# The first recurrent tile's gate products move into the four quarters of the array

## The chip, the core and the metric

The kernel runs on one NeuronCore of one Trainium2 chip. The metric is device time in microseconds (us) of one launch. A core has a matrix engine (TensorE, PE in the rows, with its weight loads as PEld), a vector engine (VectorE, DVE), a scalar engine (ScalarE, ACT), GpSimd (POOL), and a queue engine (SyncE, SP) that here only waits on semaphores and issues transfers. The five work through their own instruction lists in order and meet at semaphores.

## The reference

One layer of a hybrid decoder is computed for a prompt of 512 + 16 tokens and 8 sample streams of 8 tokens (592 token columns in all). What bears on this change is the recurrent branch:

```python
z = xn @ w_in + b_in                  # u = first 1024 columns of z
uc, _ = causal_dwconv(u, ...)         # width-4 depthwise convolution
xb = uc.reshape(B, L, 16, 64)         # 16 blocks of 64 channels
r = sigmoid(einsum('blnc,ncd->blnd', xb, w_r) + b_r)
i = sigmoid(einsum('blnc,ncd->blnd', xb, w_i) + b_i)
a = exp(-8 * r * softplus(-lam))
inp = sqrt(1 - a*a) * (i * uc)
h[t] = a[t] * h[t-1] + inp[t]         # a scan over the tokens
```

Everything else (an mLSTM branch, the merge, a ConvFFN of 2 x 2816 columns, norms) follows, and most of the time lies in its dense products.

## The kernel before

**Layout.** Features lie on the 128 partitions, tokens along the free dimension. The 1024 recurrent channels are 8 tiles u(0) to u(7) of 128 channels, each tile two of the 16 blocks. A dense product of one tile of 128 output columns (`gemm`, `split_product`) is 48 matmuls: 8 slices of the contraction, three terms each (weight high x input high, high x low, low x high), two halves of the tokens.

**Weights.** Each tile's 512 KB of weights goes through three steps. SP loads it into one of two slots of `stage` (`load`, line 569); ACT writes its rounded high part to `whi` (line 985); POOL subtracts to get the low part in `wlo` (line 927) and raises `w_lo`. Weight tile b = g + 1 belongs to the dense tile g. SP loads weight tile b only when `w_lo` says that b - 2 is split (the slot is then free). ACT takes its work in a fixed order: high part of the weight tile for g + 2, then the eviction of tile g into `u` (lines 1174 and 1176), then its share of the recurrent branch. PE starts tile g when `w_lo` counts its weights and the tile before last is evicted.

**The gates.** When u(p) is evicted, DVE convolves it into `uc[:, p]` (lines 1555 to 1560, raising `conv_done`). PE then computes the two gate products of the tile in `lru_gates(p)`, put in just ahead of dense tile `LRU_TURN[p]` (3 for p = 0, 6 for p = 1). The weights are block-diagonal, two 64 x 64 blocks per tile, in the tiles `bd[0]` (r) and `bd[1]` (i). For p = 0 the whole 128 x 128 array is used, with zeros off the diagonal: four matmuls in the code (two gates, two halves of 308 columns), which appear as eight in the trace. For p >= 1 four 64 x 64 products run side by side: the two blocks of r on the diagonal quarters, from `uc`, and the two blocks of i on the off-diagonal quarters, which take their input from a copy of `uc[:, p]` with its two halves of 64 partitions exchanged (`us[p % 2]`). The i weights of tiles 1 to 7 are therefore stored off the diagonal in `bd[1]`, those of tile 0 on it.

**The copies.** `swap_halves(p)` on SP waits until `uc[:, p]` is there, and issues two transfers (lines 660 and 661). SP's loop over g issues the weight load `main_load(g)` first (for g > 2), and then the copy whose `LRU_SWAP[p]` is g. `LRU_SWAP` is (0, 6, 7, 9, 12, 14, 16, 18), and the inner loop begins at p = 1. `main_load(3)` brings the weights (b = 4) of dense tile 3, `main_load(4)` those of tile 4, and so on. Ahead of this loop SP has stored `x_raw` to DRAM (line 636).

**PE's order in the stretch in question:** dense tiles u(1), u(2), then `lru_gates(0)`, then u(3), u(4), u(5), `lru_gates(1)`, u(6).

Of the kernel before, what the change touches and what calls it, by code (L numbers as in the profile page):

```python
# [118 lines left out]
LRU_EXP = (4, 7, 10, 12, 14, 16, 18, 20)  # L119
LRU_ROOT = (5, 8, 12, 14, 16, 18, 21, 21)  # L120
LRU_SPLIT = (6, 9, 13, 15, 17, 19, 22, 23)
LRU_SWAP = (0, 6, 7, 9, 12, 14, 16, 18)
U0 = LW - 1
US = U0 + TP
UGR = LW - 1 + LS
# [2 lines left out]
UH = UN // 2  # L128
# [124 lines left out]
def hybrid_layer(nc, a, o):  # L253
    w_in, b_in = a["w_in"][0], a["b_in"][0]
    ctx = ExitStack()
    with ctx:
        base = 16512

        def sb(name, shape, off, dt=F32):
            return nc.alloc_sbuf_tensor_at(name, shape, dt, offset=base + off)  # L260

        def sem(name):
            return ctx.enter_context(nc.semaphore(name))
# [53 lines left out]
        bd = [sb("lru_w_r", [P, 8, P], o_h + SB + 32 * UW), sb("lru_w_i", [P, 8, P], o_p + 512 * NROW + 1024)]  # L317
        uc = sb("uc", [P, 8, UN], r)
# [124 lines left out]
        bank = ctx.enter_context(nc.psum_tensor("bank", [P, 4, 512], F32))  # L443
# [18 lines left out]
        def bank2(s):  # L462

            return bank[:, 2 * s:2 * s + 2].rearrange("p h t -> p (h t)")
# [21 lines left out]
        def ffn_out(n):  # L486
# [23 lines left out]
        us_in = [sem("us_in0"), sem("us_in1")]  # L510
        bd_in, negc_ready = sem("bd_in"), sem("negc_ready")
        bd_zero, conv_done, lru_ps, lru_sig, lru_exp, lru_q, lru_sq, lru_h, lru_hi, lru_lo_ = (
            sem("bd_zero"), sem("conv_done"), sem("lru_ps"), sem("lru_sig"), sem("lru_exp"), sem("lru_q"),
            sem("lru_sq"), sem("lru_h"), sem("lru_hi"), sem("lru_lo"))
# [37 lines left out]
        def aview(ap):  # L552
            return ap.rearrange("(r c) -> r c", c=P)
# [9 lines left out]
        def _(sp):  # L563
# [39 lines left out]
            def params(arrived, group):  # L603

                for rtile, r0, src in group:
                    sp.dma_start(rows[r0:r0 + src.shape[0], rtile], src).then_inc(arrived, 16)
# [3 lines left out]
            for hf in range(2):  # L610
                lo_, hi_ = slice(BW * hf, BW * hf + BW), slice(BW - BW * hf, 2 * BW - BW * hf)
                wr, wi = (a[n][0].rearrange("(p two) c d -> two c p d", two=2)[hf] for n in ("lru_w_r", "lru_w_i"))
                sp.dma_start(bd[0][lo_, :, lo_], wr).then_inc(bd_in, 16)
                sp.dma_start(bd[1][lo_, 0:1, lo_], wi[:, 0:1]).then_inc(bd_in, 16)
                sp.dma_start(bd[1][hi_, 1:8, lo_], wi[:, 1:8]).then_inc(bd_in, 16)
            params(rows_in[1], ((1, 0, aview(a["lru_lambda"][0])), (1, 8, aview(a["mlstm_head_g"][0])),
                    (1, 16, a["state_lru_h"][0].rearrange("b (f c) -> (b f) c", c=P)),
                    (2, 0, a["state_mlstm_n"][0].rearrange("b h (i c) -> (b h i) c", c=P)),
# [24 lines left out]
            def main_load(g):  # L643

                b = B_U + g
                sp.wait_ge(w_lo, b - 1)
                if g < 16:
                    c0 = P * g if g < 8 else COL_GA + P * (g - 8)
                    load(b, b % 2, w_in, slice(c0, c0 + P))
                elif g < 24:  # L650
                    c0 = head_col(g - 16)
                    load(b, b % 2, w_in, slice(c0, c0 + P))
                else:
                    load(b, b % 2, a["w_branch_a"][0], slice(P * (g - 24), P * (g - 24) + P))
            def swap_halves(p):

                sp.wait_ge(conv_done, p + 1)
                if p >= 3:
                    sp.wait_ge(lru_ps, p - 1)
                sp.dma_start(us[p % 2][0:BW, :], uc[BW:P, p]).then_inc(us_in[p % 2], 16)  # L660
                sp.dma_start(us[p % 2][BW:P, :], uc[0:BW, p]).then_inc(us_in[p % 2], 16)

            for g in range(1, 28):
                if g > 2:
                    main_load(g)
                for p in range(1, 8):
                    if LRU_SWAP[p] == g:
                        swap_halves(p)

# [1406 lines left out]
        def _(pe):  # L2076
# [149 lines left out]
            def lru_gates(p):  # L2226

                pe.wait_ge(conv_done, p + 1)
                if p:
                    pe.wait_ge(lru_sig, p)  # L2230
                else:
                    pe.wait_ge(bd_in, 96)
                    pe.wait_ge(tile_evicted, T_U + 1)
                if p == 0:
                    for g in range(2):
                        for hf in range(2):
                            last = pe.matmul(bank[:, 2 * g + hf, 0:UH], bd[g][:, p, :], uc[:, p, UH * hf:UH * hf + UH],
                                             start=True, stop=True)
                    last.then_inc(lru_ps, 1)
                    return  # L2240

                pe.wait_ge(us_in[p % 2], 32 * ((p + 1) // 2))
                A, B = slice(0, BW), slice(BW, P)
                for hf in range(2):
                    c_ = slice(UH * hf, UH * hf + UH)
                    for g, k_, m_ in ((0, A, A), (0, B, B), (1, A, B), (1, B, A)):
                        x_ = us[p % 2][k_, c_] if g else uc[k_, p, c_]
                        last = pe.matmul(bank[m_, 2 * g + hf, 0:UH], bd[g][k_, p, m_], x_, start=True, stop=True,  # L2248
                                         tile_position=(k_.start, m_.start), skip_group_check=True)
                last.then_inc(lru_ps, 1)  # L2250

            for g in range(1, 16):
                if g in LRU_TURN:
                    lru_gates(LRU_TURN.index(g))
                gemm(B_U + g, T_U + g, (B_U + g) % 2, (T_U + g) % 2, KT, xh, xl, m0=0 if g < 8 else M0,
                     free=T_COLS2 + 1 if g == 1 else None)
# [20 lines left out]
            for n in range(8):  # L2277
                if 16 + n in LRU_TURN:
                    lru_gates(LRU_TURN.index(16 + n))
                fill(0, n)  # L2280
            for f in range(8):
# [8 lines left out]
                elif f == 6:  # L2290
                    pe.wait_ge(gates_ready, 1)
                    pe.wait_ge(lc_ready, 1)
                    for b_, r0 in ((2, 32), (3, 96)):
                        for c in range(TT):
                            last = pe.transpose(bank[:, b_, 4 * c:4 * c + HEADS], gq[r0:r0 + HEADS, P * c:P * c + P],
                                                ident[r0:r0 + HEADS, r0:r0 + HEADS])
# [187 lines left out]
            for h in range(2):  # L2484
# [17 lines left out]
                for m in range(2, 8):  # L2502
                    ffn_begin(d0 + m)
                    down_steps(m, range(HK)).then_inc(tile_done, 1)
                    if h and m == 2:

                        pe.wait_ge(tile_evicted, T_FFN + d0 + 1)
                        for n in range(FC):
                            ft, w_ = FC_SET * n, 18 * min(FC_SET, UPT - FC_SET * n)
                            last = pe.transpose(bank2(0)[0:w_, P * n:P * n + P],  # L2510
                                                flast[:, ft:ft + w_ // 18].rearrange("p f r -> p (f r)"), ident[:, :])
# [67 lines left out]
```

## Time and profile before

| | us |
|---|---|
| median of 3 runs (1062.61 to 1063.84) | 1062.91 |
| the profiled execution's own time | 1062.86 |
| its span, first to last instruction | 1061.0 |
| PE busy in the span | 1049.6 |
| DVE busy | 638.0 |
| ACT busy | 386.0 |
| POOL busy | 371.1 |

The execution whose trace is read took 1062.86 us, 1.86 us more than its span. All times in rows are counted from the start of the span. In a timeline a line gives the start, the time from there to the end of the last of the merged instructions, the engine, the line of the kernel, what is written and read, and how many instructions were merged; in brackets stands idle time before it and what ended that. SPq lines are issues of transfers: their duration is that of the issue, not of the transfer, which lands later.

### The profile page before, as it was taken

To read this page: it belongs to the slowest core of one execution; us is meant where nothing else is said; L and a number is where in the kernel's file an instruction comes from. 1 tells how busy PE (TensorE), PEld (TensorE's weight loads), DVE (VectorE), ACT (ScalarE), POOL (GpSimd) and SP (SyncE) were. 2 spreads that over 40 slices of the span, in tenths; PEclk is the share of its full clock that TensorE was granted. 3 is DMA by queue.
4 is the path that set the end of the run, shared out by engine and by line. 5 is a ranking of instruction groups with operands and counts; after the bars stand their busy time and mean duration, and the time that the engine had idled before them with its cause. 6 is when DMAs were issued, how large, how long until landed. Compare 5 with 4: busy or idle time off the path is not lost.

```text
span 1061.0 us, 19369 instructions
## 1 busy us (share of the span) xinstructions
PE 1049.6 (99%) x7924; PEld 1024.7 (97%) x7924; DVE 638.0 (60%) x975; ACT 386.0 (36%) x558; POOL 371.1 (35%) x180
## 2 busy tenths in 40 slices
PE   7999999999999999999999999999999999999997
PEld 6999999999999999999999999999999999999997
DVE  6777457964544463363643339999940189999313
ACT  6566787313333334222422343222211122222332
POOL 4333343333222222232133334444433333334430
PEclk9999999999999999999999999999999999999999
DMA  8443332376487595783452233222323222333312
GB/s 198 156 112 92 96 80 80 99 191 163 86 231 202 136 261 128 190 231 90 149 172 82 80 100 100 80 80 80 103 82 95 60 81 80 85 94 97 96 44 90
DMA packets 246465, 126.08 MB, mean 119 GB/s; under 512 B 67916, under 2 KB 242236, under 8 KB 246127
## 3 DMA queue, kind: packets, MB, share of 16 engines
q1 hardware_dynamic: 246172, 124.82, 42.8%
q8 instruction: 63, 1.03, 0.4%
q14 instruction: 20, 0.16, 0.1%
q10 hardware_dynamic: 210, 0.07, 0.0%
HBM read 100.62 MB, written 22.04 MB: 116 GB/s over the span
## 4 chain that ended last, share of the span: by engine, by line
PE 98%; ACT 1%; POOL 1%; issue 0%; DVE 0%; POOLq 0%; DVEq 0%
PE ring L2091 48%; PE ring L2480 23%; PE bank L2480 17%; PE bank L2351 2%; PE bank L2338 1%; PE bank L2138 1%; PE bank L2319 1%; PE bank L2331 1%; PE bank L2392 1%; PE bank L2248 1%; PE bank L2380 1%; POOL x_split L939 0%; PE bank L2112 0%; PE bank L2526 0%; ACT x_raw L1037 0%; ACT sq_tok L1022 0%
## 5 line engine op out<-in xcount | busy, mean ns | idle before, releaser
L2091 PE MATMUL ring<-x_split,whi 128*128 128x256 f32 (+1 forms) x2016 | 358.6, 299 | 0.0
L927 POOL TENSOR_TENSOR wlo<-stage,whi 128x1024 fp32r<-128x1024 f32 x78 | 194.8, 2497 | 405.6 <-ACT whi L985 405.6
L2091 PEld LDWEIGHTS ring<-x_split,whi 128*128 128x128 f32 x2016 | 304.3, 189 | 8.1 <-issue 7.6
L2091 PE MATMUL ring<-x_split,wlo 128*128 128x256 f32 (+1 forms) x1008 | 217.5, 297 | 0.0
L2091 PEld LDWEIGHTS ring<-x_split,wlo 128*128 128x128 f32 x1008 | 169.9, 189 | 0.0
L985 ACT ACTIVATE whi<-stage 128x1024 fp32r<-128x1024 f32 x80 | 84.3, 1053 | 97.0 <-PE ring L2091 81.0
L970 POOL TENSOR_TENSOR wlo<-stage,whi 128x1024 fp32r<-128x1024 f32 x28 | 71.1, 2539 | 108.6 <-ACT whi L1321 108.6
L2480 PE MATMUL ring<-x_split,whi 128*128 128x256 f32 (+1 forms) x512 | 88.7, 295 | 0.0
L1437 DVE SCALAR_TENSOR_TENSOR conv<-up,cols,conv 128x592 f32<-128x592 f32 x88 | 75.5, 858 | 3.1
L2480 PEld LDWEIGHTS ring<-x_split,whi 128*128 128x128 f32 x512 | 77.0, 189 | 0.0
L1997 DVE TENSOR_SCALAR conv<-up,cols 128x592 f32<-128x592 f32 x44 | 68.4, 1554 | 3.1
L2480 PE MATMUL bank<-x_split,whi 128*128 128x256 f32 (+1 forms) x384 | 66.5, 295 | 0.0
L970 POOL TENSOR_TENSOR wlo_third<-stage,whi_third 128x1024 fp32r<-128x1024 f32 x16 | 40.8, 2550 | 58.7 <-ACT whi_third L1321 58.7
L2480 PEld LDWEIGHTS bank<-x_split,whi 128*128 128x128 f32 x384 | 57.7, 189 | 0.0
L1357 ACT ACTIVATE conv<-conv 128x592 f32<-128x592 f32 x22 | 15.4, 700 | 116.3 <-DVE conv L1437 116.3
L973 POOL TENSOR_TENSOR wlo<-stage,whi 128x1408 fp32r<-128x1408 f32 x12 | 38.7, 3228 | 52.6 <-ACT whi L1323 52.6
L2480 PE MATMUL ring<-x_split,wlo 128*128 128x256 f32 (+1 forms) x256 | 54.7, 296 | 0.0
L1321 ACT ACTIVATE whi<-stage 128x1024 fp32r<-128x1024 f32 x28 | 29.5, 1054 | 61.2 <-PE ring L2480 40.4
L1838 DVE COPY num_tok<-bank 128x257 f32<-128x257 f32 x20 | 8.5, 426 | 68.7 <-PE bank L2338 60.6
L2041 DVE TENSOR_TENSOR resid<-ring,resid 128x576 f32<-128x576 f32 x9 | 6.8, 758 | 68.9 <-PE ring L2480 68.9
L2480 PE MATMUL ring<-x_split,whi_third 128*128 128x256 f32 (+1 forms) x256 | 44.6, 296 | 0.0
L2480 PE MATMUL bank<-x_split,whi_third 128*128 128x256 f32 (+1 forms) x256 | 44.4, 295 | 0.0
(364 smaller groups left out, 2063.2 us busy)
## 6 DMA issues: line engine op xcount, KB each, us to landing
stage<-in_w_in SPq DMA_DIRECT2D x56, 512.0 KB, 4.3
stage<-in_w_up SPq DMA_DIRECT2D x44, 512.0 KB, 3.8
stage<-in_w_down SPq DMA_DIRECT2D x16, 704.0 KB, 4.4
stage<-in_w_branch_a SPq DMA_DIRECT2D x8, 512.0 KB, 3.8
c_sample<-in_state_mlstm_C SPq DMA_DIRECT2D x16, 256.0 KB, 6.8
out_s_mlstm_C<-c_sample SPq DMA_DIRECT2D x16, 256.0 KB, 2.4
stage<-in_w_branch_b SPq DMA_DIRECT2D x8, 512.0 KB, 4.0
stage<-in_w_out SPq DMA_DIRECT2D x8, 512.0 KB, 3.7
```

Of the source, the lines that this page charges most:

```text
L927: pool.tensor_tensor(spaced(wlo[:, slot]), packed(stage[:, slot, 0:n]), spaced(whi[:, slot]).bitcast(F32), ALU.subtract).then_inc(w_lo, 1)
L970: pool.tensor_tensor(spaced(l_), packed(stage[:, b % 2, 0:D]), spaced(w_).bitcast(F32), ALU.subtract).then_inc(w_lo, 1)
L973: pool.tensor_tensor(l_, stage[:, b % 2, :], w_.bitcast(F32), ALU.subtract).then_inc(w_lo, 1)
L985: act.activation(spaced(whi[:, slot]), packed(stage[:, slot, 0:n]), ACT.Copy).then_inc(w_hi, 1)
L1321: act.activation(spaced(ffn_weight(i)[0]), packed(stage[:, b % 2, 0:D]), ACT.Copy).then_inc(w_hi, 1)
L1357: act.activation(cv[:, 1, 0:CV_N], cv[:, 1, 0:CV_N], ACT.Gelu_apprx_tanh).then_inc(gelu_done, 1)
L1437: return stt(out=out, in0=in0, scalar=scalar, in1=in1, op0=op0, op1=op1)
L1997: st.link(ts(c_, U[:, 0:CV_N], w[0], bias, ALU.mult, ALU.add))
L2091: last = pe.matmul(of(z, t0 or -2, t1), w[:, kk * WS:kk * WS + P], x_, start=kk == 0 and m == 0, stop=kk == kn - 1 and m == 2)
L2138: last = pe.matmul(of_first(z, t0, t1)[0:M], w[:, step * kk:step * kk + M], x[:, f, t0:t1], start=kk == 0 and m == 0, stop=kk == KT - 1 an ...
L2351: lz = pe.matmul(ZP[:, ii], kw[kappa % 3][:, P * ii:P * ii + P], vt[s][:, c, :], start=True, stop=True, skip_group_check=True)
L2480: last = pe.matmul(out(z, t0, t1), w_[:, kk * step:kk * step + P], x_[:, kk, t0 - at:t1 - at], start=kk == 0 and m == 0, stop=kk == kn - 1 ...
```

## The change

`lru_gates(0)` takes the form of the others: for each of the two halves of the tokens four quarter products, from `uc` and from a copy with exchanged halves in `us[0]`. So the copy of tile 0 is now made, at `LRU_SWAP[0] = 2`. Since `main_load` begins at g = 3, these two transfers, and the wait for `uc[:, 0]` ahead of them, stand in SP's list before `main_load(3)`. The i weights of tile 0 move off the diagonal, so that each half of `bd[1]` is loaded by one transfer instead of two (`bd_in` counts to 64, not 96). The copy of tile 2, which uses the same `us[0]` as tile 0, now waits until the gates of tile 0 are done, and the counts on `us_in` follow.

```diff
-LRU_SWAP = (0, 6, 7, 9, 12, 14, 16, 18)
+LRU_SWAP = (2, 6, 7, 9, 12, 14, 16, 18)
...
                 sp.dma_start(bd[0][lo_, :, lo_], wr).then_inc(bd_in, 16)
-                sp.dma_start(bd[1][lo_, 0:1, lo_], wi[:, 0:1]).then_inc(bd_in, 16)
-                sp.dma_start(bd[1][hi_, 1:8, lo_], wi[:, 1:8]).then_inc(bd_in, 16)
+                sp.dma_start(bd[1][hi_, :, lo_], wi).then_inc(bd_in, 16)
...
                 sp.wait_ge(conv_done, p + 1)
-                if p >= 3:
+                if p >= 2:
                     sp.wait_ge(lru_ps, p - 1)
...
             for g in range(1, 28):
                 if g > 2:
                     main_load(g)
-                for p in range(1, 8):
+                for p in range(8):
                     if LRU_SWAP[p] == g:
                         swap_halves(p)
...
-                    pe.wait_ge(bd_in, 96)
+                    pe.wait_ge(bd_in, 64)
                     pe.wait_ge(tile_evicted, T_U + 1)
-                if p == 0:
-                    for g in range(2):
-                        for hf in range(2):
-                            last = pe.matmul(bank[:, 2 * g + hf, 0:UH], bd[g][:, p, :], uc[:, p, UH * hf:UH * hf + UH],
-                                             start=True, stop=True)
-                    last.then_inc(lru_ps, 1)
-                    return
-
-                pe.wait_ge(us_in[p % 2], 32 * ((p + 1) // 2))
+                pe.wait_ge(us_in[p % 2], 32 * (p // 2 + 1))
```

## Rows read from the trace of the kernel before

**Rows 1.** The page, part 4: the chain that ended last, by engine.

```profile
PE 98%; ACT 1%; POOL 1%; issue 0%; DVE 0%; POOLq 0%; DVEq 0%
```

**Rows 2.** Waits of PE, whole span: waiting line, cause, total us, times, longest.

```profile
PE ring L2107 <- POOL misc L906: 2.9, 1, 2.9
PE bank L2138 <- POOL wlo_third L945: 1.0, 1, 1.0
```

**Rows 3.** Timeline of PE, 47 to 49.6 us: gates of tile 0.

```profile
47.18 0.44 PE L2091 MATMUL ring<-x_split,wlo 128*128 128x272 f32 x2
...
49.30 0.52 PE L2091 MATMUL ring<-x_split,whi 128*128 128x272 f32 x1
```

**Rows 4.** Timeline of PE, 68 to 74 us: gates of tile 1.

```profile
69.02 0.44 PE L2091 MATMUL ring<-x_split,wlo 128*128 128x272 f32 x2
69.38 0.48 PE L2248 MATMUL bank<-uc,lru_w_r 64*64 64x308 f32 x2
...
70.58 0.82 PE L2091 MATMUL ring<-x_split,whi 128*128 128x272 f32 x4
```

**Rows 5.** Timeline of SP: issues of an i load, the store of x_raw, a copy.

```profile
13.57 0.62 SPq L615 DMA_DIRECT2D lru_w_i<-in_lru_w_i  x1
...
24.79 0.36 SPq L636 DMA_DIRECT2D x_turned<-x_raw  x1
...
51.69 0.59 SPq L660 DMA_DIRECT2D uc_swapped<-uc  x1
52.32 0.60 SPq L661 DMA_DIRECT2D uc_swapped<-uc  x1
```

**Rows 6.** Timeline of SP, narrow windows: issues of weights of tiles 3 and 4.

```profile
31.05 0.40 SPq L569 DMA_DIRECT2D stage<-in_w_in  x1
...
38.09 0.37 SPq L569 DMA_DIRECT2D stage<-in_w_in  x1
```

**Rows 7.** Waits of SP, 25 to 60 us.

```profile
SPq L569 <- POOL wlo L927: 32.0, 5, 7.1
```

**Rows 8.** Timeline of DVE, 24 to 120 us: convolutions of u(0), u(1); an idle.

```profile
40.24 2.65 DVE L1437 SCALAR_TENSOR_TENSOR uc<-u,cols,uc 128x616 f32<-128x616 f32 x3
43.04 0.18 DVE L1555 COPY stage<-u 128x27 f32<-128x27 f32 x1
...
60.42 0.80 DVE L1580 TENSOR_TENSOR lru_r<-u 128x616 f32<-128x616 f32 x1 [5.44 <-ACT u L1134]
```

**Rows 9.** Timeline of ACT, 24 to 62 us: high part for tile 3, then eviction of u(1).

```profile
41.15 1.07 ACT L985 ACTIVATE whi<-stage 128x1024 fp32r<-128x1024 f32 x1 [4.63 <-PE ring L2091]
42.11 0.69 ACT L1174 ACTIVATE u<-ring,cols 128x528 f32<-128x528 f32 x1
```

**Rows 10.** Timeline of POOL, 24 to 115 us: low parts for tiles 2, 3 and 7.

```profile
35.66 2.41 POOL L927 TENSOR_TENSOR wlo<-stage,whi 128x1024 fp32r<-128x1024 f32 x1 [4.64 <-ACT whi L985]
42.29 2.87 POOL L927 TENSOR_TENSOR wlo<-stage,whi 128x1024 fp32r<-128x1024 f32 x1 [4.23 <-ACT whi L985]
...
70.68 2.95 POOL L927 TENSOR_TENSOR wlo<-stage,whi 128x1024 fp32r<-128x1024 f32 x1 [3.96 <-ACT whi L985]
```

**Rows 11.** Issue to landing (last number), issues at 45.19, 31.05, 51.27, 51.69, 1.67.

```profile
stage<-in_w_in SPq DMA_DIRECT2D x1, 512.0 KB, 3.8
...
stage<-in_w_in SPq DMA_DIRECT2D x1, 512.0 KB, 5.8
...
stage<-in_w_in SPq DMA_DIRECT2D x1, 512.0 KB, 4.9
uc_swapped<-uc SPq DMA_DIRECT2D x1, 154.0 KB, 4.6
...
x_tok<-in_x_prompt SPq DMA_DIRECT2D x1, 512.0 KB, 5.0
```

**Rows 12.** Stretches: us, PE, PEld, DVE, ACT, POOL busy, granted clock, DMA share, GB/s.

```profile
0.00:5.00 5.00, 2.14 (x10) 2.12 (x11) 1.82 (x2) 1.49 (x2) 3.41 (x19) 1.00 0.58 178
...
45.50:46.00 0.50, 0.50 (x6) 0.50 (x5) 0.47 (x2) 0.00 (x0) 0.00 (x0) 1.00 0.00 0
```

## The prediction

> **What bounds the kernel now.** I read the chain of work that ended last first: 98% of it is PE [rows 1]. So the question for every edit is what it does to PE's order of work, and time saved on another engine is worth nothing by itself. Then the waits of PE: nearly all of its idle time lies in the first 15 us, a first wait of 2.9 us and one of 1.0 us being the longest [rows 2]. From there on PE goes from tile to tile without a gap, so any gap that the change opens ahead of a dense tile is added to the end in full, and any matmul time that it saves there is taken off in full. Last I read the timelines of SP, ACT, POOL, DVE and PE between 24 and 75 us side by side, because the change does not only reshape a product: it puts a wait and two transfers into SP's list ahead of the weights of dense tile 3.
>
> **Part 1, the products themselves.** From the start of the last two dense matmuls ahead of the gates of tile 0 to the first dense matmul behind them is 47.18 to 49.30, 2.12 us [rows 3]. The same distance around the gates of tile 1, which already run in quarters and have the same 308 columns, is 69.02 to 70.58, 1.56 us [rows 4]; what the change of form costs on either side is inside it. The new form is thus worth 2.12 - 1.56 = 0.56 us of PE, if nothing else is late.
>
> **Part 2, the weights' loads.** Two issues of 0.62 us [rows 5] fall away and the bytes stay. What follows on SP comes some 1.3 us sooner, until SP next waits: the store of x_raw at 24.79 waits for ACT's copies, and the weight loads from 31.05 on wait for POOL (five waits, 32.0 us together) [rows 5 to 7]. No wait of PE is ended by any of these transfers [rows 2]. I cost this at 0.
>
> **Part 3, the copy of tile 0 ahead of the load for tile 3.** This is the part that decides. SP now has, right behind the store of x_raw, a wait until uc of tile 0 is complete, then two issues, and only then the load of weight tile 4 for dense tile 3. Before, that load was issued at 31.05, when POOL had freed its slot [rows 6, 7]. Now:
>
> - DVE's convolution of u(0) ends at 40.24 + 2.65 = 42.89 [rows 8]. It depends on nothing that moves. SP reacts within about 0.03 us (POOL ends at 35.66 + 2.41 = 38.07 and SP issues at 38.09 [rows 6, 10]): 42.92.
> - First copy to second copy 0.63 us (51.69 to 52.32), then 0.60 us and a gap of 0.05 [rows 5]: the load is issued at 44.20. It is 13.15 us later than before.
> - Landing. A load with nothing beside it took 3.8 us, one with two copies right behind it 4.9, one that met the tail of the x_raw store 5.8 [rows 11]. Ours has 308 KB of copies ahead and the load for tile 4, whose slot has been free since 38.07, 0.4 us behind it. The nearest row is the x_tok load of 512 KB that stood in a queue with transfers on both sides: 5.0 us [rows 11]. I take 5.0 and keep 3.8 and 5.8 as ends: landed at 49.20.
> - ACT's high part to POOL's start is 41.15 to 42.29, 1.14 us [rows 9, 10]; POOL takes 2.41 us, against 2.95 in its slowest row here [rows 10]; the hand-overs at both ends are 0.02 each. PE can start tile 3 at 49.20 + 0.02 + 1.14 + 2.41 + 0.02 = 52.79.
>
> Before, tile 3 started at 49.30 [rows 3]. The cover that the load had was large: ACT could start on these weights only when PE had left their slot at 41.15 [rows 9], and POOL had them split by 42.29 + 2.87 = 45.16 [rows 10], 4.1 us ahead of need. A delay of 13.15 us uses all of this up and leaves 52.79 - 49.30 = 3.49 us of idle PE. With a landing of 3.8 us it is 2.3; with 5.8 and POOL's 2.95 it is 3.49 + 0.8 + 0.54 = 4.8.
>
> The 0.56 us of part 1 is not to be taken off again: the gates are done within the wait. PE has a wait of its own there, for the copy. The second transfer is issued at 43.55 and a copy beside a load landed in 4.6 us [rows 11], so at 48.15 at the latest. Queued behind this wait on PE is everything else; but the products take 69.38 to 70.58, 1.20 us [rows 4], and end by 49.35, over 3 us ahead of the weights. This wait is hidden by the late load. Without that cover it would cost 49.35 - 49.30 = 0.05 us at worst, and at best the full 0.56 us would be gained.
>
> The Trainium skill has a price for a landing: "DMA: Bandwidth & Descriptors", section "Anatomy of one DMA — SWDGE (gpsimd) path", fits 2.0 us plus the bytes over 436 GB/s, by which I estimate 3.2 us for 512 KB. By it tile 3 would start at 50.99 and the loss would be 1.7 us. The trace has 3.8 us for the undisturbed load, and on another queue than that section's, so the row decides.
>
> **What else stands behind the late load.** ACT's list is fixed: the eviction of u(1), right behind the high part for tile 3 and begun at 42.11 [rows 9], with DVE taking it up at 43.04 [rows 8], now runs from some 50.3 to 51.2. PE asks for it before tile 3, but the low part at 52.79 is later. The load for tile 4 is issued at 44.6 instead of 38.09; its high part follows that eviction and is done near 52.3, its low part near 55.2. PE wants it after tile 3, at 52.8 + 6.6 = 59.4 (three dense tiles fill 49.30 to 69.30 [rows 3, 4]): 4 us to spare, so there is no second gap. DVE starts the convolution of u(1) about 8 us later than its 43.04, at 51.3, and what it then did until its idle before 60.42 took at most 60.42 - 5.44 - 43.04 = 11.9 us [rows 8], so it is through by 63.2. The input that ended that idle comes from ACT behind PE's tile 3 and moves to about 63.9. So DVE is back in step. The copy of tile 1 leaves near 57 and lands near 62, with PE wanting it at 69.38 + 3.5 = 72.9. Everything behind tile 3 then runs as before, 3.5 us later.
>
> **The sum.** The profiled execution took 1062.86 us with a span of 1061.0; the median of the runs is 1062.91, so the two can stand for one another. 1062.86 + 3.49 = 1066.4 us. With the ends of the landing and of POOL's step: 1065.2 to 1067.7.
>
> **Rival A, nothing is late (it ends as no change).** If the weights for tile 3 still arrived in time, the new form would give between +0.05 and -0.56 us: 1062.3 to 1062.9, say 1062.6. For this the load would have to be issued by 49.30 - (3.8 + 0.02 + 1.14 + 2.41 + 0.02) = 41.91 even with the fastest landing, so the convolution of u(0) would have to end near 40.6 instead of 42.89. For it speaks the long cover of 10 us between issue and need; against it, that the convolution alone ends later than this point, with 1.3 us of issues still to come. Chance 0.06.
>
> **Rival B, a short landing.** A load that was issued at 45.19 with nothing queued moved no byte until 46.00 [rows 11, 12], 0.8 us. Behind the copies, with the engines already at work, this start could be hidden: a landing of 3.8 - 0.8 = 3.0 us, a loss of 3.49 - 2.0 = 1.5 us, 1064.4 us, which is inside 0.2%. Against it speaks that the copies take engine time themselves, and that no weight load in the rows is under 3.8 us. Chance 0.10.
>
> **Rival C, the clock.** The granted clock is 1.00 in every stretch that I looked at, the 2.4 GHz level, even in the first 5 us where PE was busy for 2.14 us only [rows 12]. The longest idle of PE, 2.9 us, stands ahead of its first matmul [rows 2]. The change leaves PE idle from its gates (48.7 to 49.35) to 52.8, 3.4 to 4.1 us in one piece, behind dense work; the trace has no such place. If the clock falls to 1.2 GHz, dense work takes twice as long until it rises. Between no matmul and the whole of tile 3 at that level the price is 0 to 6.6 us; I take half the tile, 3.3 us: 1066.4 + 3.3 = 1069.7 us. The Trainium skill, "TensorE: Matmul & The Clock Gate", section "HAM oscillation — how this bites in real kernels", describes just that: a wait between bursts of matmuls sends the clock back to the low level. No row here shows it. Chance 0.10.
>
> **How the numbers follow.** The forecast has the remaining 0.74. About 0.2%, 2.1 us, is what a measurement of this kernel can tell from no change; 1065.0 is that point. The forecast's own range, 1065.2 to 1067.7, is above it; rival C too: slower 0.84. Rivals A and B lie within: 0.15, and 0.01 is left for faster. The range that should hold the time 8 times in 10 reaches from rival B's 1064.4 to the forecast's upper end, 1067.8, and leaves out rivals A and C and a rest of the forecast.
>
> **What would show it.** On SP the two copies at 42.9 and 43.5 and the load for tile 3 near 44.2 (instead of 31.05); on ACT an idle until about 49.2 that a transfer ends, then the high part, with the eviction of u(1) behind it; on PE two new idle times, a short one ahead of the gates or none, and one of over 3 us ahead of tile 3 that POOL's low part ends; the gates in 1.2 us. From tile 4 on the distances between tiles should be the old ones. The prediction is wrong if the idle ahead of tile 3 is under 2 us, if a second gap follows at tile 4, 5 or at the gates of tile 1, or if the granted clock is under 1.00 behind the idle.

## The result and the profile after

The changed kernel took 1066.97 us (median of 6 runs, 1065.72 to 1069.14) against 1062.87 us before (6 runs): a ratio of 1.004, with an interval of 1.003 to 1.005. It is 4.1 us slower. What the slowest run, 1069.14, met is not known. The profiled execution took 1066.73 us with a span of 1064.9. In it everything up to the gates of tile 0 lies some 0.45 us earlier than in the execution shown of before, because the first rows of x landed earlier (ACT's first work on them starts at 4.90 instead of 5.38 us); distances, not times, are compared below.

The timeline of PE, with the gates of tile 0 at line 2239 and the dense tiles at line 2090 (in brackets idle time and what ended it):

```profile
46.73 0.44 PE L2090 MATMUL ring<-x_split,wlo 128*128 128x272 f32 x2
47.10 0.48 PE L2239 MATMUL bank<-uc,lru_w_r 64*64 64x308 f32 x2
...
51.42 1.33 PE L2090 MATMUL ring<-x_split,whi 128*128 128x272 f32 x4 [3.06 <-POOL wlo L926]
52.55 0.70 PE L2090 MATMUL ring<-x_split,wlo 128*128 128x272 f32 x2
...
55.25 0.44 PE L2090 MATMUL ring<-x_split,wlo 128*128 128x272 f32 x2
...
72.55 0.44 PE L2090 MATMUL ring<-x_split,wlo 128*128 128x272 f32 x2
...
74.11 0.67 PE L2090 MATMUL ring<-x_split,whi 128*128 128x272 f32 x3
```

From the last dense pair to the start of tile 3 it is now 46.73 to 51.42, 4.69 us, where it was 2.12 [rows 3]: 2.57 us lost. PE stands idle for 3.06 us, until POOL's low part is there; the products in front are shorter, which is why the loss is smaller than the idle. And the first matmuls of tile 3 are slow: the pair at 52.55 takes 0.70 us, that at 55.25 the usual 0.44. Why, the stretches show (us; busy time of PE, PEld, DVE, ACT, POOL; granted clock; DMA share; GB/s):

```profile
50.00:51.00 1.00, 0.00 (x0) 0.00 (x0) 1.00 (x1) 1.00 (x2) 1.00 (x1) 1.00 0.00 0
51.00:52.00 1.00, 0.58 (x2) 0.58 (x3) 0.96 (x2) 0.98 (x3) 1.00 (x2) 0.74 0.00 0
52.00:53.00 1.00, 1.00 (x5) 1.00 (x5) 1.00 (x1) 0.99 (x2) 1.00 (x1) 0.50 0.32 56
53.00:54.00 1.00, 1.00 (x5) 1.00 (x5) 1.00 (x1) 1.00 (x2) 0.94 (x1) 0.50 1.02 296
54.00:55.00 1.00, 1.00 (x6) 1.00 (x6) 0.96 (x2) 0.92 (x2) 0.00 (x0) 0.55 0.60 173
55.00:56.00 1.00, 1.00 (x9) 1.00 (x9) 0.96 (x2) 0.00 (x0) 0.00 (x0) 1.00 0.82 156
```

The granted clock is 0.50, the 1.2 GHz level, from the start of tile 3 until shortly before 55 (the stretches from 51 and from 54 us hold some time at either level, hence 0.74 and 0.55). Tile 3's start to the last pair ahead of the gates of tile 1 is 51.42 to 72.55, 21.13 us, where it was 49.30 to 69.02, 19.72 [rows 3, 4]: 1.41 us more. Around the gates of tile 1 it is 72.55 to 74.11, the old 1.56 us.

So two losses, 2.57 and 1.41 us, 3.98 together, against the measured 4.1. (The two profiled executions differ by 3.9 in span: 3.98 less the 0.45 us of the earlier start, and 0.35 us of one further wait of PE at 245.8 us, which a second profile of this kernel, below, does not have.)

Where the idle comes from is seen on SP, ACT and POOL, one timeline each; the fourth fence is the view of landings for what was issued from 43.4 to 43.8 us (last number, us from issue to landing):

```profile
42.46 0.51 SPq L659 DMA_DIRECT2D uc_swapped<-uc  x1
43.01 0.60 SPq L660 DMA_DIRECT2D uc_swapped<-uc  x1
43.65 10.68 SPq L569 DMA_DIRECT2D stage<-in_w_in  x4
```

```profile
47.87 1.06 ACT L984 ACTIVATE whi<-stage 128x1024 fp32r<-128x1024 f32 x1 [11.81 <-DMA stage<-in_w_in]
48.84 0.68 ACT L1173 ACTIVATE u<-ring,cols 128x528 f32<-128x528 f32 x1
```

```profile
49.01 4.93 POOL L926 TENSOR_TENSOR wlo<-stage,whi 128x1024 fp32r<-128x1024 f32 x2 [11.40 <-ACT whi L984]
```

```profile
stage<-in_w_in SPq DMA_DIRECT2D x1, 512.0 KB, 4.2
uc_swapped<-uc SPq DMA_DIRECT2D x1, 154.0 KB, 2.5
```

The load for tile 3 is the first of the four merged lines at 43.65; before it went out at 31.05 [rows 6]. ACT waits 11.81 us for its landing where it used to wait for PE [rows 9], POOL follows at 49.01, and 2.41 us later PE starts. The copies land in 2.5 us, at 45.5, ahead of the gates at 47.10: PE does not wait for them.

### The profile page after: what moved, and what is told of

Read it like the earlier page. It is cut to its first block, busy times and chain, and to the rows that moved or that the text cites. A ratio compares the mean times of both kernels' runs of the same rounds, so it can differ in the third digit from the quotient of the medians.

```text
span 1064.9 us, 19387 instructions
## 1 busy us (share of the span) xinstructions
PE 1049.9 (99%) x7932; PEld 1025.2 (96%) x7932; DVE 635.7 (60%) x975; ACT 385.5 (36%) x558; POOL 370.5 (35%) x180
## 4 chain that ended last, share of the span: by engine, by line
PE 77%; issue 16%; POOL 5%; ACT 1%; DVE 0%; POOLq 0%; DVEq 0%
PE ring L2090 30%; PE ring L2471 22%; PE bank L2471 17%; POOL wlo L926 4%; PE bank L2342 2%; PE bank L2329 1%; PE bank L2310 1%; PE bank L2322 1%; PE bank L2383 1%; PE bank L2371 1%; POOL x_split L938 0%; PE bank L2111 0%; PE bank L2517 0%; ACT x_raw L1036 0%; ACT x_split L1048 0%
```

## The experiments

Two theories stood at first. One: all of the loss comes from the place of the copy in SP's list, through the late load and what the idle does to the clock. The other: the quarter form of the first tile, its weights or the copies' traffic cost something by themselves.

**The copy behind the load for tile 4.** One number of the changed kernel.

```diff
-LRU_SWAP = (2, 6, 7, 9, 12, 14, 16, 18)
+LRU_SWAP = (4, 6, 7, 9, 12, 14, 16, 18)
```

> The changed kernel with one number different: the copy of tile 0 is issued behind the load for dense tile 4 (g = 4) instead of ahead of the load for tile 3. Theory (the loss is the late load of tile 3's weights and what follows from it): the load is issued near 31 again, tile 3 starts 1.56 us behind the start of the last two dense matmuls ahead of the gates plus at most 0.6 for the copy, no idle ahead of tile 3, clock 1.00; 1062.3 to 1062.9 us, up to 0.6 us faster than before. Rival (the quarter form of the first tile, or the i weights' load, costs something itself): it stays near 1066 to 1067.

Measured: 1062.11 us (11 runs) against 1062.69 for the kernel before, run beside it; ratio 0.9995 (0.9986 to 1.0004). The timeline of PE:

```profile
47.05 0.44 PE L2090 MATMUL ring<-x_split,wlo 128*128 128x272 f32 x2
...
48.61 0.83 PE L2090 MATMUL ring<-x_split,whi 128*128 128x272 f32 x4
```

1.56 us from pair to tile, the distance of the gates of tile 1, no idle. With everything of the change but its place in SP's list, the whole loss is gone. The first theory holds.

**The wait alone.** One line in the kernel before, ahead of SP's loop of loads; no copy, the old products.

```diff
+            sp.wait_ge(conv_done, 1)
             for g in range(1, 28):
                 if g > 2:
                     main_load(g)
```

> The kernel before with one line more: SP waits until uc of tile 0 is there, ahead of the load for tile 3. No copies, the gates of tile 0 in the old form. Theory (the place in SP's order): the load is issued near 42.9, lands in 3.8 to 4.2 us, tile 3 starts near 50.5 instead of 49.3, an idle of about 1.2 us, too short to lower the clock: about 1064.1 us. Rival (the wait is harmless and the copies' traffic beside the load is what delays it): 1062.9, no idle ahead of tile 3.

Measured: 1063.85 us (10 runs) against 1062.69; ratio 1.001 (1.0001 to 1.0019). PE, then SP:

```profile
48.07 0.44 PE L2092 MATMUL ring<-x_split,wlo 128*128 128x272 f32 x2
...
51.43 0.82 PE L2092 MATMUL ring<-x_split,whi 128*128 128x272 f32 x4 [0.85 <-POOL wlo L928]
```

```profile
43.81 10.55 SPq L569 DMA_DIRECT2D stage<-in_w_in  x4
```

This execution lies 0.9 us later as a whole; the distance is 3.36 us, 1.24 more than before, and the time moved by 1.16. A single wait on the queue engine, with nothing added to do, costs about a microsecond here (by the interval, 0.1 to 2.0 us). The clock stays at 1.00.

**The copy early, the old products.** The changed kernel with the gates of tile 0 on the full array and the i weights loaded as before (the lines for the weights are left out below).

```diff
                 pe.wait_ge(us_in[p % 2], 32 * (p // 2 + 1))
+                if p == 0:
+                    for g in range(2):
+                        for hf in range(2):
+                            last = pe.matmul(bank[:, 2 * g + hf, 0:UH], bd[g][:, p, :], uc[:, p, UH * hf:UH * hf + UH],
+                                             start=True, stop=True)
+                    last.then_inc(lru_ps, 1)
+                    return
```

> The changed kernel with the copy in its early place, but the gates of tile 0 in the old form on the full array (and the i weights loaded as before); the copy of tile 0 is made and waited for, and not used. Tile 3 must start at the same distance as in the changed kernel, 4.7 us behind the start of the last dense pair, with PE idle 0.56 us less, about 2.5 us. If the clock falls only after the longer idle: clock 1.00 behind it and about 1065.0 us, so the faster products would have cost more than they saved. If it falls here too: 1066.5 to 1067.

Measured: 1065.65 us (7 runs, 1064.76 to 1067.08) against 1062.69; ratio 1.0029 (1.0017 to 1.004). PE, and one stretch in the columns used above:

```profile
47.02 0.44 PE L2091 MATMUL ring<-x_split,wlo 128*128 128x272 f32 x2
...
51.81 0.82 PE L2091 MATMUL ring<-x_split,whi 128*128 128x272 f32 x4 [2.28 <-POOL wlo L927]
```

```profile
52.00:53.00 1.00, 1.00 (x8) 1.00 (x8) 0.96 (x2) 1.00 (x1) 1.00 (x1) 1.00 0.25 36
```

The distance is 4.79 us, near the 4.69 of the changed kernel, and the clock is 1.00 behind the idle in the profiled execution (1065.19 us). The slower products end in the same wait. The faster ones of the changed kernel brought nothing there and left a longer idle, behind which the clock fell. (The two slowest of the seven runs here, 1066.55 and 1067.08 us, may have seen a fall too; they have no profile. Their mean clock, 0.998 against 0.999 in the others, does not decide it: the mean of a run takes in a fall behind the last matmul, where nothing is left to be slowed, as shown at the end, and 16 of 70 runs of the kernel before have 0.997 or 0.998.)

**Dense matmuls in the wait.** The changed kernel with matmuls that nobody reads ahead of the gates of tile 0, 15 of them in the first variant, 6 in the second.

```diff
                 pe.wait_ge(us_in[p % 2], 32 * (p // 2 + 1))
+                if p == 0:
+                    for n in range(FILL):
+                        pe.matmul(bank[:, n % 4, 0:2 * P], xh[:, n % 8, 0:P], xh[:, n % 8, 0:2 * P],
+                                  start=True, stop=True)
```

> The changed kernel with 15 dense matmuls of 256 columns more on PE, whose result nobody reads, ahead of the gates of tile 0, about 2 us. They fit into the time in which PE waits for the weights of tile 3, so tile 3 starts at the same distance (4.7 us behind the last dense pair), with an idle of about 1.1 us left. Theory (the low clock at tile 3 follows from the idle and costs about 1.4 us): clock 1.00 throughout, near 1065.3 us. Rival (the low clock has another cause, or costs nothing): near 1066.9 as the changed kernel.

Measured with 15: 1065.00 us (10 runs, 1064.52 to 1066.01) against 1062.69; ratio 1.0022 (1.0012 to 1.0031). PE:

```profile
46.80 0.44 PE L2091 MATMUL ring<-x_split,wlo 128*128 128x272 f32 x2
47.08 1.98 PE L2237 MATMUL bank<-x_split 128*128 128x256 f32 x15
...
51.62 0.82 PE L2091 MATMUL ring<-x_split,whi 128*128 128x272 f32 x4 [1.36 <-POOL wlo L927]
```

A stretch of it, in the columns used above:

```profile
52.00:53.00 1.00, 1.00 (x10) 1.00 (x9) 1.00 (x1) 0.99 (x2) 1.00 (x1) 1.00 0.21 35
```

Two microseconds of added matmuls make the kernel faster than the changed one by 1.4 to 1.8 us: it lies 2.31 us above the kernel before that ran beside it, the changed kernel 3.68 (below) and 4.10 above its own. Tile 3 starts at about the same distance (4.82), and its clock is 1.00. What the low clock costs is shown.

> The changed kernel with 6 instead of 15 dense matmuls of 256 columns, unread, ahead of the gates of tile 0: 0.8 us, so that the idle ahead of tile 3 is about 2.3 us, as long as that of the kernel with the old gate products, but behind quarter products. Theory (the length of the idle decides): clock 1.00 behind it, 1065.0 to 1065.3 us. Rival (quarter products count for less, and the clock falls because they stand ahead of the idle): the clock falls as in the changed kernel and the time is near 1066.7.

Measured with 6: 1066.43 us (8 runs) against 1062.94; ratio 1.0027 (1.0016 to 1.0038). Its runs fall into two groups by time: five of 1066.38 to 1066.88 us, three of 1064.80 to 1065.13 (mean granted clock 0.997 and 0.999). The profiled one is of the first group; PE, and a stretch (us, PE busy, granted clock, DMA share, GB/s):

```profile
51.90 1.24 PE L2091 MATMUL ring<-x_split,whi 128*128 128x272 f32 x4 [2.46 <-POOL wlo L927]
```

```profile
53.00:54.00 1.00, 1.00 (x6) 0.50 0.81 171
```

The rival's reading came true in the profiled run and, by the times, in five of the eight. The groups lie 1.7 us apart (the middles, 1066.70 and 1064.99), a little more than one fall of the clock costs in the traces: from the start of tile 3 to the last pair ahead of the gates of tile 1 it is 21.13, 21.01 and 21.12 us in the three profiles with a fall (the changed kernel twice and this one), 1.3 to 1.4 us more than the 19.72 of before. Six profiles of other kernels here without a fall have 19.55 to 19.72.

**A longer idle behind the old products.** The kernel with the early copy and the full array, with the copy of tile 0 made once more into the other buffer, so that the load goes out 1.3 us later.

```diff
+                if p == 0:
+                    sp.dma_start(us[1][0:BW, :], uc[BW:P, p]).then_inc(us_extra, 16)
+                    sp.dma_start(us[1][BW:P, :], uc[0:BW, p]).then_inc(us_extra, 16)
+                elif p == 1:
+                    sp.wait_ge(us_extra, 32)
                 sp.dma_start(us[p % 2][0:BW, :], uc[BW:P, p]).then_inc(us_in[p % 2], 16)
```

> The kernel with the early copy and the old gate products on the full array, with the copy made twice (once more into the second buffer, unread), so that the load for tile 3 is issued 1.2 us later still and the idle ahead of tile 3 grows from 2.3 to about 3.5 us. Theory (the length of the idle decides): the clock is 0.50 at the start of tile 3, and to the 1.2 us of idle come some 1.4 us: 1068 us or a little more. Rival (the clock falls only behind the quarter products): clock 1.00, 1066.9 us.

Measured: 1067.20 us (5 runs, 1066.47 to 1067.81) against 1062.94; ratio 1.004 (1.0025 to 1.0054). The profiled one took 1066.47 us; PE, and a stretch:

```profile
52.84 0.82 PE L2097 MATMUL ring<-x_split,whi 128*128 128x272 f32 x4 [3.45 <-POOL wlo L933]
```

```profile
53.00:54.00 1.00, 1.00 (x8) 1.00 0.17 16
```

An idle of 3.45 us, longer than any other here, and the clock at 1.00 behind it. The theory that the length of the idle alone decides falls. Whether the three slower runs, 1067.20 to 1067.81 us, saw a fall is not shown: the five spread over 1.34 us, and the 19 of the kernel before beside them over 1.22.

**The changed kernel again**, beside these.

> The changed kernel itself, once more, beside the other kernels of this call and on their chip. Theory: an idle of about 3 us ahead of tile 3, clock near 0.50 at its start, 1066.5 to 1067.5 us. If the fall of the clock were chance, this execution would show 1.00 and about 1065.3 us.

Measured: 1066.62 us (5 runs, 1066.33 to 1067.42) against 1062.94; ratio 1.0037 (1.0022 to 1.0051). PE, and a stretch:

```profile
51.46 1.36 PE L2090 MATMUL ring<-x_split,whi 128*128 128x272 f32 x4 [3.02 <-POOL wlo L926]
```

```profile
52.00:53.00 1.00, 1.00 (x6) 0.50 0.39 52
```

The fall is there again, behind 3.02 us of idle. All eleven runs of this kernel have a mean clock of 0.996 to 0.998, where the kernel before has 0.999 or more in 54 of 70: the fall is seen in both profiles and likely in most of the other runs.

**The copy behind the load for tile 3.** `LRU_SWAP` begins with 3 instead of 2, so that the load for tile 4 is the one held back.

> The changed kernel with the copy of tile 0 behind the load for tile 3 and ahead of the load for tile 4 (g = 3). The load for tile 4 is then the one that waits, to about 44.2 instead of 38.1. Theory (only the load whose cover is smaller than the delay costs time): landed by 48.4, its high part follows the eviction of u(1) at about 47.6 to 48.5 and then 49.5, low part by 52, wanted at about 55.3: hidden; 1062.1 us, as with the copy behind load 4. Rival (any load held for the copy costs): an idle ahead of tile 4 and 1063 to 1065 us.

Measured: 1062.18 us (10 runs) against 1062.94; ratio 0.9992 (0.9982 to 1.0002). SP, then PE:

```profile
31.25 0.39 SPq L569 DMA_DIRECT2D stage<-in_w_in  x1
43.16 0.51 SPq L659 DMA_DIRECT2D uc_swapped<-uc  x1
43.71 0.60 SPq L660 DMA_DIRECT2D uc_swapped<-uc  x1
44.35 8.37 SPq L569 DMA_DIRECT2D stage<-in_w_in  x3
```

```profile
47.42 0.44 PE L2090 MATMUL ring<-x_split,wlo 128*128 128x272 f32 x2
...
48.98 0.83 PE L2090 MATMUL ring<-x_split,whi 128*128 128x272 f32 x4
```

The same wait of SP, one load later, costs nothing: the load for tile 4, issued at 44.35 instead of 38.1, is still in time.

**The second part of the change alone, and the last kernel once more.** The first of these two loads the i weights of each half in two transfers again.

```diff
-                sp.dma_start(bd[1][hi_, :, lo_], wi).then_inc(bd_in, 16)
+                sp.dma_start(bd[1][hi_, 0:1, lo_], wi[:, 0:1]).then_inc(bd_in, 16)
+                sp.dma_start(bd[1][hi_, 1:8, lo_], wi[:, 1:8]).then_inc(bd_in, 16)
...
-                    pe.wait_ge(bd_in, 64)
+                    pe.wait_ge(bd_in, 96)
```

> The kernel with the copy behind the load for tile 3, and the i weights of each half loaded by two transfers again (tile 0, then tiles 1 to 7), all off the diagonal. It differs from the next kernel by the second part of the change alone. Theory (nothing waits for these issues): the same time as that one, 1062.2 us, within 0.2. Rival (two issues of 0.6 us less ahead of the first stores and loads are worth something): 0.3 to 1.3 us slower than the next.

> The kernel with the copy behind the load for tile 3 once more, for its interval against the kernel before. By the distance on PE, 1.56 us instead of 2.12 around the gates of tile 0, it should be 0.56 us faster: a ratio of 0.9995. If the gain of the products were eaten elsewhere, the ratio would be 1.000.

Measured: 1062.08 us with two transfers, 1062.20 with one (11 runs each), against 1062.67; ratios 0.9995 (0.9986 to 1.0004) and 0.9996 (0.9987 to 1.0005). The single transfer is worth nothing that shows. With the copy behind load 3 or 4 the four medians lie 0.47 to 0.76 us below those of before, around the 0.56 us that the distance on PE gives; each interval still takes in 1, so the gain is shown on PE and not, clear of noise, in the time.

## Why the prediction was right, and where it was not

The time (1066.97 us against 1066.4), the side and the place were as forecast. The sum was not: 3.49 us of idle stood for 2.57 of idle and 1.41 of low clock. Its two errors, of opposite sign, nearly cancelled, so that the time came out so close is luck. (The forecast's upper end stands there as 1067.7 and as 1067.8; by its terms it is 1067.7.)

- **What bounds the kernel, and that SP's order decides:** right. A gap ahead of a dense tile went to the end in full: 1.24 us on PE gave 1.16 in time with the wait alone.
- **Part 1, 0.56 us for the products:** right, 1.56 us of distance in both kernels with the copy placed later; and right that it is lost in the changed kernel.
- **Part 2 at nothing:** right.
- **Part 3, the wait of SP, the two issues, ACT and POOL:** right. The convolution ended at 42.43 in the profiled execution, the load went out at 43.65, 1.22 later (the sum had 1.31); ACT's start to POOL's start was 1.14 us, as put, and POOL's start to PE's 2.41, where the sum had 2.43. The end of the convolution:

```profile
39.78 2.65 DVE L1436 SCALAR_TENSOR_TENSOR uc<-u,cols,uc 128x616 f32<-128x616 f32 x3
```

- **The landing, 5.0 us:** mis-sized. It was 4.2. The row that I judged nearest, an x_tok load between others, stood in a far fuller queue (448 KB were issued at 1.21 us ahead of it and two more loads of 512 KB right behind it), which is the likely reason; no run tests it. The copies had no load ahead of them and landed in 2.5 us, not in the 4.6 of a copy issued behind a load [rows 11]. With that the idle added to the end is 2.57 us instead of 3.49, within the bounds of 2.3 to 4.8. The fit that the Trainium skill has in "DMA: Bandwidth & Descriptors", section "Anatomy of one DMA — SWDGE (gpsimd) path", gave an estimate of 3.2 us; the trace differs, and the measured 4.2 decides.
- **The copies' own wait on PE:** none, where up to 0.7 us was allowed for.
- **ACT, DVE, and no second gap:** right. Tile 4 and the gates of tile 1 follow without idle, and DVE's next input from ACT came at 63.94 (forecast 63.9):

```profile
63.94 0.80 DVE L1579 TENSOR_TENSOR lru_r<-u 128x616 f32<-128x616 f32 x1 [3.39 <-ACT u L1133]
```

- **Rival C, the clock, at a chance of 0.10:** this is the step that failed, and a clock under 1.00 behind the idle stood among the prediction's own signs of being wrong. The sum put the cost of the clock at nothing. It was held to be an alternative to the forecast and it came on top of it, in both profiles of the changed kernel. The evidence that I set against it, a clock of 1.00 in the first 5 us [rows 12], says nothing on an idle behind dense work, which I had noted, and should have weighed. That no row shows such a fall was true of the rows read, not of the trace: at its end, behind PE's last matmul, the trace of before has one (last section). The price put on rival C, half a tile or 3.3 us, was too high: 1.41 us in the profile, 1.4 to 1.8 us by the filler, 1.7 between the two groups of the 6-matmul kernel. Rivals A and B did not come; the time of A, 1062.6 us, is near that of the kernels with the copy placed later.

Without the fall of the clock I estimate the changed kernel at 1065.2 to 1065.4 us (1062.87 and the 2.31 us of the kernel with 15 unread matmuls, or the 2.57 of the idle): close above 1065.0, which the prediction took as the edge of what can be told from no change.

## What to carry to other kernels

A wait that is put into a queue engine's list holds back everything behind it: before placing one, write down when each load behind it is issued now, when it is needed, and the work between landing and need. The same copy one place later costs nothing, since the load it then delays has the cover. And where a wait sets the end, making the work in front of it faster is worth nothing, and can cost: here the faster products left PE idle for 3.06 us instead of 2.28, and in the profiles the clock was low behind that idle and not behind the other.

## What was not expected of the hardware

The granted clock fell to 0.50 behind a wait of 3.06 and of 3.02 us and stayed there for some 3 us of dense work. The Trainium skill, "TensorE: Matmul & The Clock Gate", section "HAM oscillation — how this bites in real kernels", describes such falls behind waits, and the trace agrees that they happen. But the length of the idle does not order the profiles: the clock fell behind 2.46 us of idle with quarter products ahead of it (and by the times in five of the eight runs of that kernel), and stayed at 1.00 behind 3.45 us with full-array products ahead. Behind 1.36 us with quarter products and 2.28 us with full-array ones it did not fall in the profile. That quarter products ahead of an idle make a fall likelier would fit all of these, but no run here shows it by itself; it stays open, as does what separates the two groups of runs of one and the same kernel.

The clock also falls where no time is lost by it, behind the last matmul. Two kernels with the same matmuls at their end, the kernel before and then the one with the copy behind load 4, in the columns used above:

```profile
1055.00:1060.00 5.00, 0.15 (x2) 0.00 (x0) 0.88 (x2) 0.74 (x2) 0.00 (x0) 0.95 0.95 347
1060.00:1065.00 5.00, 0.00 (x0) 0.00 (x0) 0.00 (x0) 0.00 (x0) 0.00 (x0) 0.69 0.00 1
```

```profile
1050.00:1055.00 5.00, 4.57 (x42) 4.31 (x41) 4.17 (x9) 3.56 (x8) 0.00 (x0) 1.00 0.50 173
1055.00:1060.00 5.00, 0.00 (x0) 0.00 (x0) 0.43 (x1) 0.35 (x1) 0.00 (x0) 0.67 0.84 299
```

PE ends at 1055.15 and the clock falls near 1059.5 us in the first, 1054.57 and 1056.6 in the second. So even behind the same work the fall does not come equally soon in every execution, which would fit the two groups of runs of one kernel; no run here tests that.
